# Convolution feed-forward: one 512-column matmul for both activation halves, the second half of the bank copied by ScalarE and added by VectorE

## What is computed

```python
def conv_ffn(x, w_up, conv_w, conv_b, w_down):
    h = x @ w_up                                   # (256, 1024) @ (1024, 5632)
    C = h.shape[-1]
    h = lax.conv_general_dilated(h, conv_w[:, None, :].astype(h.dtype), window_strides=(1,),
                                 padding=[(CONV_WIDTH - 1, 0)], ...,
                                 feature_group_count=C) + conv_b
    gate, up = jnp.split(h, 2, axis=-1)
    return (jax.nn.silu(gate) * up) @ w_down       # (256, 2816) @ (2816, 1024)
```

## Time and profile before

| | |
|---|---|
| time, median of 3 runs (lowest, highest) | 1730.21 us (1728.34, 1730.79) |
| the profiled execution: its time, its span | 1731.79 us, 1730.0 us |
| mean granted TensorE clock | 0.98 |
| busy: PE, PEld, DVE, ACT | 1665.5, 1528.9, 1139.6, 890.6 us |
| first convolution feed-forward, about | 159 to 348 us of the span |
| second, about | 476 to 665 us |

### The profile page before, as it was taken

One profiled execution on the slowest core, in us unless ns is written; L12 is line 12 of the kernel. 1 busy time (PEld: TensorE's weight loads), 2 busy tenths in 40 slices (PEclk: granted clock), 3 DMA queues, 4 the chain that ended last, 5 costly groups with the idle time before them and its releaser, 6 DMA issues.

```text
span 1730.0 us, 32525 instructions
## 1 busy us (share of the span) xinstructions
PE 1665.5 (96%) x12061; PEld 1528.9 (88%) x12061; DVE 1139.6 (66%) x1899; ACT 890.6 (51%) x1419; POOL 26.2 (2%) x72
## 2 busy tenths in 40 slices
PE   7999999998999998999999999999899999999998
PEld 7888999886799997999889889998899998689997
DVE  4768877775577777555656875556765557565555
ACT  6455655654465556444466464444644445464443
POOL 4000000000000000000000000000000000000000
PEclk9999999997999999999999999999999999799999
DMA  9446666573266666666665546666466665136662
GB/s 249 140 133 195 197 185 185 172 148 94 77 183 182 183 187 212 195 186 188 184 207 157 184 145 196 184 187 187 132 190 187 184 182 159 49 115 195 186 187 82
DMA packets 393755, 292.73 MB, mean 169 GB/s; under 512 B 33403, under 2 KB 365588, under 8 KB 393296
## 3 DMA queue, kind: packets, MB, share of 16 engines
q1 hardware_dynamic: 390160, 279.79, 55.8%
q0 software_dynamic: 2816, 10.24, 1.7%
q10 hardware_dynamic: 704, 1.67, 0.3%
HBM read 290.59 MB, written 1.07 MB: 169 GB/s over the span
## 4 chain that ended last, share of the span: by engine, by line
PE 90%; DVE 6%; ACT 2%; issue 1%; DMA 1%; SPq 0%; DVEq 0%; ACTq 0%
PE ps L391 28%; PE ps L392 28%; PE ps L393 28%; DVE w_lo L382 1%; DVE SQ L571 1%; DVE H L578 1%; PE ps L1982 1%; PE ps L1981 1%; DMA raw<-in_hgrn_w_in 1%; PE ps L892 0%; PE ps L1433 0%; PE ps L459 0%; PE ps L1704 0%; DVE A L1613 0%; ACT x_hi L472 0%
## 5 line engine op out<-in xcount | busy, mean ns | idle before, releaser
L391 PE MATMUL ps<-x_hi,w_hi 128*128 128x256 f32 x2672 | 762.9, 286 | 9.5 <-DVE x_lo L501 5.5
L392 PE MATMUL ps<-x_hi,w_lo 128*128 128x256 f32 x2672 | 758.9, 284 | 0.0
L393 PE MATMUL ps<-x_lo,w_hi 128*128 128x256 f32 x2672 | 758.9, 284 | 0.0
L382 DVE TENSOR_TENSOR w_lo<-raw,w_hi 128x1024 fp32r<-128x1024 f32 x532 | 646.6, 1219 | 33.5 <-ACT w_hi L375 32.8
L375 ACT ACTIVATE w_hi<-raw 128x1024 fp32r<-128x1024 f32 x532 | 542.5, 1046 | 83.2 <-PE ps L393 74.1
L391 PEld LDWEIGHTS ps<-x_hi,w_hi 128*128 128x128 f32 x2672 | 515.4, 193 | 18.3 <-issue 10.6
L392 PEld LDWEIGHTS ps<-x_hi,w_lo 128*128 128x128 f32 x2672 | 515.5, 193 | 4.4
L393 PEld LDWEIGHTS ps<-x_lo,w_hi 128*128 128x128 f32 x2672 | 515.2, 193 | 0.0
L695 ACT ACTIVATE sl<-gs 128x256 f32<-128x256 f32 x88 | 36.9, 419 | 399.7 <-DVE gs L800 399.7
L800 DVE TENSOR_TENSOR gs<-ps,R 128x256 f32<-128x256 f32 x88 | 37.3, 424 | 275.9 <-PE ps L393 275.9
L391 PE MATMUL ps<-w_hi,h_hi 128*128 128x512 f32 x528 | 207.2, 392 | 2.1 <-DVE h_lo L724 2.1
(11 more groups left out here) (281 smaller groups left out, 1280.5 us busy)
## 6 DMA issues: line engine op xcount, KB each, us to landing
raw<-in_ffn_w_up SPq DMA_DIRECT2D x176, 512.0 KB, 3.8
raw<-in_ffn_w_down SPq DMA_DIRECT2D x132, 512.0 KB, 4.5
raw<-in_ffn_w_gate SPq DMA_DIRECT2D x88, 512.0 KB, 4.7
raw<-in_hgrn_w_in SPq DMA_DIRECT2D x32, 512.0 KB, 4.8
raw<-in_gmlp_w_in SPq DMA_DIRECT2D x32, 512.0 KB, 4.3
raw<-in_gmlp_w_out SPq DMA_DIRECT2D x16, 512.0 KB, 3.7
raw<-in_hgrn_w_out SPq DMA_DIRECT2D x8, 512.0 KB, 3.5
raw<-in_dsa_w_in SPq DMA_DIRECT2D x16, 256.0 KB, 4.6
```

The lines of the kernel that those rows point to most:

```text
L382: nc.vector.tensor_tensor(w_lo[:, s, :], raw[:, s, :], w_hi[:, s, :].bitcast(F32), ALU.subtract)\
L391: pe.matmul(o, whi, xhi, start=first, stop=False, skip_group_check=not group)
L392: pe.matmul(o, wlo, xhi, start=False, stop=False, skip_group_check=not group)
L393: return pe.matmul(o, whi, xlo, start=False, stop=last, skip_group_check=not group)
```

## The change

In the convolution feed-forwards the high weights are loaded once for a k-step and stream `x_hi` and `x_lo` together as 512 columns. To this end the two lie side by side in one buffer `x_both`. The low weights then stream `x_hi` as 256 columns into the first half of the bank. So a k-step has two matmuls in place of three, and the bank holds two halves that are yet to be added. ScalarE copies the second half to SBUF (`half`, into `SQ`), VectorE adds it to the first into `gs` or `us`, and multiplies by `R` in an instruction of its own from SBUF. TensorE now waits for the sums (`gate_sum`, `up_sum`). The plain feed-forwards, and all other stages, keep their instructions; only the buffer that they read x from has another layout.

```diff
-        x_hi = sb("x_hi", [P, KT, L], F32R)
-        x_lo = sb("x_lo", [P, KT, L], F32R)
+        x_both = sb("x_both", [P, KT, 2, L], F32R)
+        x_hi, x_lo = x_both[:, :, 0, :], x_both[:, :, 1, :]
...
+        def feat_pair(pe, o, c0, x_wait=None):
+
+            s = c0 % RING
+            whi, wlo = wv(s, KT)
+            for k in range(KT):
+                if x_wait is not None:
+                    pe.wait_ge(*x_tiles("x_lo_done", x_wait, k + 1))
+                pe.matmul(o, whi[:, k, :], x_both[:, k, :, :].rearrange("p a l -> p (a l)"), start=k == 0, stop=False,
+                          skip_group_check=True)
+                last = pe.matmul(o[:, 0:L], wlo[:, k, :], x_hi[:, k, :], start=False, stop=k == KT - 1, skip_group_check=True)
+            return last
...
-            gate_read, up_read = ("gate_read", "up_read") if conv else ("plain_gs", "hid")
+            gate_read, up_read = ("gate_sum", "up_sum") if conv else ("plain_gs", "hid")
...
+            def half(i, n, i0, what, read, done):
+
+                act.wait_ge(used, tile_chunk(c0, i0) + what + 1 + RING * n)
+                if i0 > 0:
+                    act.wait_ge(*tile(read, f, i))
+                nc.scalar.activation(SQ[:, what, :], ps[:, 2 * (i0 % 2) + what, L:2 * L], ACT.Copy).then_inc(S(done), 1)
+
             def it(i, n, i0):
                 par = i0 % 2
                 c = tile_chunk(c0, i0) + HI_AHEAD
                 split_hi(act, c, n)
+                if conv:
+                    half(i, n, i0, 0, "gate_sum", "gate_half")
...
                 split_hi(act, c + 1, n)
                 if conv:
+                    half(i, n, i0, 1, "up_sum", "up_half")
                     act.wait_ge(*tile("up_read", f, i + 1))
...
-                gate_at = c + 1 + RING * n
-                dve.wait_ge(used, gate_at)
-                nc.vector.tensor_tensor(gs[:, par, :], ps[:, 2 * par, 0:L], R[:, :], ALU.mult).then_inc(S("gate_read"), 1)
+                dve.wait_ge(*tile("gate_half", f, i + 1))
+                nc.vector.tensor_tensor(gs[:, par, :], ps[:, 2 * par, 0:L], SQ[:, 0, :], ALU.add).then_inc(S("gate_sum"), 1)
                 if i0 > 0:
                     up_first(i)
+                dve.wait_ge(*tile("gate_sum", f, i + 1))
+                nc.vector.tensor_tensor(gs[:, par, :], gs[:, par, :], R[:, :], ALU.mult).then_inc(S("gate_read"), 1)
                 split_lo(dve, c + AHEAD, n)
...
-                dve.wait_ge(used, gate_at + 1)
-                nc.vector.tensor_tensor(us[:, :], ps[:, 2 * par + 1, 0:L], R[:, :], ALU.mult).then_inc(S("up_read"), 1)
+                dve.wait_ge(*tile("up_half", f, i + 1))
+                nc.vector.tensor_tensor(us[:, :], ps[:, 2 * par + 1, 0:L], SQ[:, 1, :], ALU.add).then_inc(S("up_sum"), 1)
+                dve.wait_ge(*tile("up_sum", f, i + 1))
+                nc.vector.tensor_tensor(us[:, :], us[:, :], R[:, :], ALU.mult).then_inc(S("up_read"), 1)
```

More of the change, by code:

```diff
@@ L629, in up_part @@
                         pe.wait_ge(*tile(read, f, i - 1))
-                    mm = feat_tile(pe, ps[:, 2 * par + what, 0:L], c + what,
-                                   x_wait=n_ if i0 == 0 and what == 0 else None)
+                    xw = n_ if i0 == 0 and what == 0 else None
+                    if not conv:
+                        mm = feat_tile(pe, ps[:, 2 * par + what, 0:L], c + what, x_wait=xw)
+                    else:
+                        mm = feat_pair(pe, ps[:, 2 * par + what, :], c + what, x_wait=xw)
                     mm.then_inc(used, 1)
```

## The result

The changed kernel takes **1785.19 us** (median of 4 runs, 1782.32 to 1790.38) where the kernel before takes 1730.5 us. The ratio is 1.0315, 95% interval 1.0295 to 1.0335: **slower by some 54 us**. 1783.0 was forecast. The profiled execution took 1790.38 us with a span of 1788.6 us, against 1730.0 before.

The account below looks back on a forecast made before the run. Bound: PE before, then the 9.42 us ScalarE-VectorE round. Per convolution feed-forward +8.4, +16.6 and +1.1 us, 52.2 for both, on 1731.79; less 1.6 to the median, plus 0.3 clock each: 1783.0 us, range 1770 to 1802.

Parts of the forecast that it names:

- The bound: Convolution feed-forwards: PE sets the pace before the change without a gap, at 8.50 us a tile.
- the round: Loop of convolution feed-forwards: ScalarE and VectorE steps, tied twice a tile, last 9.42 us against PE's new 8.31.
- the last part of the prediction: Signs expected in the profile: gate sums 3 and 21 169 to 170 us apart, PE idle about 1.1 us a tile.
- One sign of being wrong: Prediction fails if time has gone to a stage outside the two convolution feed-forwards.
- The bounds for hand-overs that no row had shown: Unknown waits in the loop: -10 us at the low end, +9 us and 6 us of clock at the high.
- The PE term: PE in convolution feed-forwards: k-step 0.348 us instead of 0.36, so 0.19 us less a tile, 8.31 instead of 8.50.
- rows 2: Profile rows of PE before: two 256-column matmuls start 0.12 us apart, 512-column ones take 0.228 us each.
- rival 1: Convolution feed-forwards: PE keeps the pace and becomes faster, twice 2.4 us gained, 1725.4 us; chance 7%.
- The spacing rule: Skill's matmul distance, columns over 2.4 GHz plus 2.5 ns: a merge worth 0.0025 us, 1.8 us in all.
- Start, middle, end: Each convolution feed-forward: +8.4 us to tile 3, +16.6 over 18 tiles, +1.1 from gate 21 to residual.
- The clock: PE gaps lower no clock mid-layer, perhaps at the end: 0 to 3 us a convolution feed-forward, 0.3 taken.
- More than a weight split too long: Argument against PE keeping the pace: the loop's summed steps would have to be 1.11 us too long.

Follow-up runs that it names:

- three_tied: Changed kernel with TensorE back at three 256-column matmuls a k-step, one into the bank's second half; ratio 1.0301 to the kernel before.
- pair_no_tie: Kernel before with only the changed kernel's TensorE work and buffer; the bank's second half is never read; ratio 0.9979, 8.387 us a tile.
- grouped_no_tie: As pair_no_tie, but eight 512-column matmuls first, then eight 256-column ones, instead of in turn; ratio 0.9968 to the kernel before, 8.307 us a tile.
- layout_only: Kernel before with only x_hi and x_lo placed side by side in one buffer; ratio 1.0004 to the kernel before.

## Why the prediction was right, point by point

**The bound.** "PE sets the pace there without a gap", and the round takes its place: right. After the change the copies run right behind a weight split, VectorE waits for them, and PE for `w_lo`, each as the last part of the prediction had said. The sums of gate tiles 3 and 21 are 168.6 us apart where 169 to 170 was said, and PE stands idle for `w_lo` for 0.7 to 0.8 us a tile by the rows, which count from the modelled end of the matmul ahead, or 0.9 by the distance of starts, where 1.1 was said. One sign of being wrong was time outside the two feed-forwards: 8.7 of the 58.6 us between the profiles lie there, and some 5 of the 54.7 between the medians. three_tied and the pair of moved copies show that it is the round and its order, not the work.

**The round.** Forecast 9.42 us, measured 9.366. Step by step from the two timelines above: copy to sum 0.40 (0.42 forecast), sum to multiplication 0.46 (0.46), `ua` behind it 0.60 (0.60), first of the two splits to the copy 1.89 (1.90), silu to split 0.32 (0.32), split to copy 0.95 (0.95). The copy took 0.36 us and not the 0.38 of the earlier trace rows, twice in a round; the rest is rounding. The bounds for hand-overs that no row had shown were not needed: the sums start 0.04 us behind the end of their copy and the multiplication of the up half 0.04 behind the end of its sum (324.22 to 324.26), and 0.18 stands only in front of `ua`, the instruction that reads its column from a register, as before. (The bounds themselves add up to 1798 at the top, 9 and 6 above 1783.0, and not 1799.)

**The PE term.** Too large: 0.19 us a tile was taken off, 0.113 is what pair_no_tie shows (8.500 - 8.387). The step that was off is "form and length are those of rows 2, so I take their price": it held for matmuls of one width in a row (grouped_no_tie: 8.307), but not for the order in turn without gaps (8.387), and in the changed kernel for a part of the tiles only. There it hides behind the round and does not touch the forecast. It would have shown in rival 1, whose 1725.4 would have been about 1729.

The spacing rule of the Trainium skill ("TensorE: Matmul & The Clock Gate", section "Back-to-back issue gap") gave 0.0025 us a merge; the page gives it for the isolated matmul. Measured are 0.007 in turn without gaps and 0.012 grouped, so the trace does not agree: the rule is on the low side here in both orders.

**Start, middle, end.** +8.4, +16.6 and +1.1 us were forecast, +8.2, +15.6 and +1.1 came: 24.9 for a layer against 26.1. The forecast of 1783.0 lies 2 us below the median of 1785.2. That it is this close is in part luck: it has 2.9 us too much for the two layers (2.3 in the rounds, 0.6 for the clock), and lacks some 5 us outside them. From the profiles alone I cannot tell what those 5 are; layout_only leaves at most 2.4 of them to the buffer, and they are no larger than what the start of the kernel varies by from one profile to the next (168.1 to 173.5 us).

**The clock.** In the middle it stayed at its upper level, as said, and at the end it fell. Two windows of the changed kernel (stretch and its length; busy us and count of PE, of its weight loads, of VectorE, ScalarE and GpSimd; granted clock; DMA share and GB/s):

```profile
330.00:360.00 30.00, 27.81 (x143) 22.86 (x144) 23.68 (x44) 16.98 (x30) 0.00 (x0) 1.00 0.51 155
...
370.00:374.00 4.00, 3.46 (x8) 2.81 (x9) 2.64 (x7) 3.03 (x5) 0.00 (x0) 0.50 0.64 175
```

and PE's wait for `h_lo` of tile 20, forecast as 4 us:

```profile
370.55 0.77 PE L391 MATMUL ps<-w_hi,h_hi 128*128 128x512 f32 x1 [3.79 <-DVE h_lo L749]
```

From 370 to 374 us the granted clock is 0.50, the lower level of 1.2 GHz, behind this wait. It costs next to nothing, as the end from gate to residual is VectorE's and took 13.64 us where 13.67 was forecast.

**The rivals.** Rival 1 had PE keep the pace. That came with both copies ahead of their splits, though not faster than before (+0.8 us a layer), and with the addition in VectorE alone. "More than a weight split too long" was right: with the gate's split passed the round is 8.42, still above PE's 8.39, and only with both passed is it below, at 8.10.

## What to carry to other kernels

When a change puts a hand-over between two engines into a loop, add up the closed round from start to start in program order, on both engines, and compare it with the bound; how busy the engines are says nothing about it (VectorE was busy for 23.7 of 30 us and ScalarE for 17.0 while they set the pace). If the round is too long, look in it for a long instruction that nobody in the round needs, here a weight split ahead of a short copy, and move the copy ahead: the two moves took the loss from 54.5 us down to 2.9 (ratios 1.0315 and 1.0017). Better still, here, was to let the engine that needs the sum make it alone (0.9953 in all six layers), and to run matmuls of the same width one behind the other (0.9869 with both).

## What was not expected of the hardware

- Matmuls of 512 and of 256 columns, both with a weight load of their own, cost 0.353 us a pair in turn and without gaps, and 0.349 grouped by eights (8.387 against 8.307 us a tile, in six layers 8.3 us between the two sums of the traces). In turn but with a gap in each tile, in the middle of the changed kernel's first layer, they cost 0.347 in one tile and 0.353 in the next. Why, no run here shows.
- VectorE's `tensor_reduce` over pairs 256 elements apart in a PSUM bank, 512 in and 256 out, takes 0.69 us from start to end. The sum with ScalarE's copy takes 0.42, 0.27 less of VectorE, but needs the copy.
- ScalarE's copy of 128 x 256 from PSUM took 0.36 us where the like one in the attention takes 0.38 (means 0.362 of 88 and 0.383 of 13 in the same profile).
